# A new order of the weight stream, norm sums on VectorE, and another prelude in a hybrid decoder layer

## The reference

```python
x = x + 0.5 * swiglu_ffn(rms_norm(x, ffn1_norm), ffn1_w_gu, ffn1_w_down)      # width 5632
p = rms_norm(x, mix_norm) @ w_in       # ua, va, glu_a, glu_b, gate_a, gate_b, each 2048 wide
# A: u = gelu(ua); v = layer_norm(gelu(va)); y_a = (u * (tril(W_s) v + b_s)) @ w_pa per chunk of 128
# B: g = glu_a * sigmoid(glu_b); c = silu(layer_norm(causal depthwise conv, width 31, of g)); y_b = c @ w_pb
x = x + (sigmoid(gate_a) * y_a + sigmoid(gate_b) * y_b) @ w_out
x = x + 0.5 * swiglu_ffn(rms_norm(x, ffn2_norm), ffn2_w_gu, ffn2_w_down)
y = rms_norm(x, final_norm)            # rms_norm(x, g) = x * rsqrt(mean(x*x) + eps) * g
```

## Time and profile before

| | before |
|---|---|
| time, median of 3 runs | 3491.16 us (3490.33 to 3492.99) |
| profiled execution, its own time | 3496.27 us |
| its span, first to last instruction of the slowest core (core 2) | 3494.7 us |
| spans of the 8 cores | 3480.9 to 3494.7 us |
| PE busy | 3253.0 us (93%), 21555 matmuls |
| DVE busy | 856.9 us (25%) |
| ACT busy | 466.4 us (13%), 29 table loads |
| transfers | 284.30 MB, mean 81 GB/s |
| mean granted clock of TensorE, core 2 | 0.966 |

### The profile page before, as it was taken

The page is one execution under the profiler, slowest core; times in us unless marked ns, Lnnn a source line. Parts: engine busy times, 40 slices in busy tenths (PEclk is TensorE's granted clock), DMA queues, the critical chain, the costliest instruction groups (busy, mean ns, idle before and its releaser), DMA issues.

```text
span 3494.7 us, 51300 instructions; the slowest of 8 cores (3480.9 to 3494.7 us)
## 1 busy us (share of the span) xinstructions
PE 3253.0 (93%) x21555; PEld 2067.1 (59%) x21556; DVE 856.9 (25%) x1448; ACT 466.4 (13%) x909; POOL 128.1 (4%) x246
## 2 busy tenths in 40 slices
PE   6999999999999756579899999999999999999997
PEld 2566666666665434347756666666666666666664
DVE  2212122121126221222643111112412112112115
ACT  3000000000003100014721000000300000000002
POOL 0000000000000000000000000000000000000000
PEclk9999999999999878789999999999999999999998
DMA  6436434334345343352344334337333434434434
GB/s 155 74 61 123 80 59 81 69 66 85 66 103 127 67 85 55 78 115 59 65 87 73 71 70 71 71 69 177 58 72 71 84 63 78 73 58 82 73 63 119
DMA packets 74112, 284.30 MB, mean 81 GB/s; under 512 B 9888, under 2 KB 36768, under 8 KB 52000
## 3 DMA queue, kind: packets, MB, share of 16 engines
q0 software_dynamic: 34848, 216.62, 35.6%
q1 hardware_dynamic: 39040, 64.40, 6.3%
HBM read 468.14 MB, written 32.87 MB: 143 GB/s over the span
## 4 chain that ended last, share of the span: by engine, by line
PE 91%; DMA 5%; DVE 2%; ACT 1%; issue 1%; POOL 0%; SPq 0%; DVEq 0%; ACTq 0%; POOLq 0%
PE ps L192 91%; DMA arena<-w_glu 4%; ACT arena L195 1%; DVE arena L205 1%; DMA arena<-xin 1%; ACT L195 0%; DVE arena L209 0%; DVE arena L198 0%; DMA vsamp<-arena 0%; DMA arena<-gd 0%; POOL arena L949 0%; DMA gd<-arena 0%; SPq L949 0%; DVEq L940 0%; DVE arena L201 0%
## 5 line engine op out<-in xcount | busy, mean ns | idle before, releaser
L192 PE MATMUL ps<-arena 128*128 128x364 bf16 (+5 forms) x21555 | 3253.0, 313 | 220.7 <-DMA arena<-w_glu 141.6
L192 PEld LDWEIGHTS ps<-arena 128*128 128x128 bf16 (+1 forms) x21556 | 2067.1, 98 | 1406.5 <-issue 282.4
L198 DVE TENSOR_TENSOR arena<-arena,ps 128x364 bf16<-128x364 f32 (+9 forms) x472 | 237.0, 515 | 1838.9 <-PE ps L192 1836.4
L195 ACT ACTIVATE arena<-ps 128x364 f32<-128x364 f32 (+1 forms) x528 | 241.5, 463 | 2574.4 <-PE ps L192 2524.5
L205 DVE SCALAR_TENSOR_TENSOR arena<-ps,arena 128x364 f32<-128x364 f32 (+5 forms) x451 | 241.1, 539 | 501.2 <-PE ps L192 500.9
L198 DVE TENSOR_TENSOR arena<-arena 128x512 bf16<-128x512 f32 (+7 forms) x168 | 185.3, 1115 | 67.3 <-PE ps L192 44.2
L195 ACT ACTIVATE arena<-arena 128x364 bf16<-128x364 f32 (+6 forms) x276 | 152.8, 631 | 268.5 <-PE ps L192 191.7
L205 DVE SCALAR_TENSOR_TENSOR arena<-arena 128x364 bf16<-128x364 f32 (+4 forms) x196 | 101.2, 594 | 1.8 <-DVE arena L209 0.2
L949 POOL DMA_DIRECT2D arena<-w_gu x88 | 46.6, 529 | 1173.3 <-PE ps L192 1132.8
L949 POOL DMA_DIRECT2D arena<-w_dn x64 | 33.8, 528 | 773.8 <-PE ps L192 761.6
L195 ACT ACTIVATE arena<-ps,arena 128x272 bf16<-128x272 f32 (+3 forms) x76 | 38.0, 500 | 102.9 <-PE ps L192 102.8
(11 more groups left out here) (10 smaller groups left out, 15.9 us busy)
## 6 DMA issues: line engine op xcount, KB each, us to landing
arena<-w_gu POOLq DMA_DIRECT2D x88, 1024.0 KB, 8.1
arena<-w_dn POOLq DMA_DIRECT2D x64, 704.0 KB, 6.2
arena<-w_glu POOLq DMA_DIRECT2D x16, 1024.0 KB, 11.7
arena<-w_gate POOLq DMA_DIRECT2D x16, 1024.0 KB, 8.7
arena<-w_pab POOLq DMA_DIRECT2D x16, 1024.0 KB, 9.8
arena<-w_v POOLq DMA_DIRECT2D x8, 1024.0 KB, 9.6
arena<-w_u POOLq DMA_DIRECT2D x8, 1024.0 KB, 8.1
arena<-w_out POOLq DMA_DIRECT2D x8, 1024.0 KB, 10.3
```

The source lines that it names most:

```text
L192: return P.op("pe", lambda e: e.matmul(out, lhsT, rhs, start=start, stop=stop), deps)
L195: return P.op("act", lambda e: e.activation(out=out, in_=in_, func=func, **kw), deps)
L198: return P.op("dve", lambda e: e.tensor_tensor(out=out, in0=in0, in1=in1, op=op), deps)
```

## The change

Three parts. (1) `wseq` lists all weight tiles in the order of use, `wissue` issues the next one, `wnext` hands out the oldest issued one, and `wdone` releases a slot and issues the next tile at once, at that place of POOL's list. (2) The mixer's, the second FFN's and the final norm use `RowNorm`: each row is squared on ACT as soon as it is made, and DVE adds the squares into ACC (f32); before the last row the sum is split into two bf16 parts, which two matmuls against ONES sum over the partitions, and the last row's square is a third one. The 16 scalings stand in `norm_rows`, as before. (3) In the prelude segment 1's tokens are loaded behind segment 0's, the weight loads wait for other pieces of the tokens, `warm` puts small matmuls ahead of segment 0's sums and 30 behind them, the first unit of each segment interleaves gate and up matmuls (`paced`), and the order of the first nine units is another.

```diff
-        def wload(src, n, after=()):
-            idx, slot, free = wring.get()
-            ev = P.dma("pool", slot[:, 0:n], src, "w%d" % idx, deps=free + list(after))
-            return idx, slot, ev
+        def wissue(after=()):
+            if wseq:
+                src, n = wseq.pop(0)
+                idx, slot, free = wring.get()
+                wahead.append((idx, slot, P.dma("pool", slot[:, 0:n], src, "w%d" % idx, deps=free + list(after))))
+        def wnext():
+            return wahead.pop(0)
+        def wdone(idx, events):
+            wring.release(idx, events)
+            wissue()
...
         load_tokens(0)
         ev_pv = P.dma("sp", PV, pv_d, "c_pv")
+        load_tokens(1, [x_ev[(0, 3)]])
+        def warm(n):
+            bi, bk, bfree = banks.get()
+            lm = None
+            for i in range(n):
+                lm = mm(bk[:, 0:128], ONES, ONES, True, True, deps=[e_ones] + (bfree if i == 0 else []))
+            banks.release(bi, [lm])
...
+                    if nwarm:
+                        warm(nwarm)
                     lm = mm(bk[:, 0:n], ONES, sq[:, 0:n], k == 0, k == KC - 1, deps=[ea, e_ones] + bfree)
...
+        class RowNorm:
+            def add(self):
+                if not self.sqs:
+                    return
+                (si, sq, ea) = self.sqs.pop(0)
+                if self.ev is None:
+                    self.ev = ts(self.acc, sq, 1.0, 0.0, ALU.mult, ALU.add, deps=[ea])
+                else:
+                    self.ev = tt(self.acc, self.acc, sq, ALU.add, deps=[ea, self.ev])
+                SQR.release(si, [self.ev])
+            def row(self, k, dep):
+                self.add()
+                self.square(k, dep)
+            def split(self):
+                e1 = ts(hi[:, 0:n], self.acc, 1.0, 0.0, ALU.mult, ALU.add, deps=[self.ev] + hf)
+                e2 = tt(lo[:, 0:n], self.acc, hi[:, 0:n], ALU.subtract, deps=[e1] + lf)
+            def sum_parts(self):
+                l1 = mm(bk[:, 0:n], ONES, hi[:, 0:n], True, False, deps=[e1, e_ones] + bfree)
+                l2 = mm(bk[:, 0:n], ONES, lo[:, 0:n], False, False, deps=[e2])
+            def finish(self):
+                lm = mm(self.bank[1][:, 0:self.n], ONES, sq, False, True, deps=[ea])
+                norm_rows(gidx, Xs, Hout, self.x0, self.n, s, self.bank, lm, out)
...
                     for s in range(3):                        # last three down tiles, held
                         for (mp, wi, slot, lev) in held:
                             for mi in range(2):
-                                ld, ed = down(W, mp * 2 + mi, mi, s, lev)
-                                if s > 0:
-                                    run_steps(tail_steps[s - 1], 3)
+                                m = mp * 2 + mi
+                                if m == 10 and s == 0:
+                                    for q in range(3):
+                                        norms[q].add()
+                                if m == 15:
+                                    norms[s].add()
+                                    norms[s].split()
+                                ld, ed = down(W, m, mi, s, lev)
+                                if m == 15:
+                                    norms[s].sum_parts()
+                                    norms[s].square(m, ed)
+                                else:
+                                    norms[s].row(m, ed)
+                                if s > 0 and m == 10:
+                                    norms[s - 1].finish()
...
             if what == "w":
-                return [] if i == 0 else [x_ev[(i - 1, 3)]]
-            if what == "wl" and i < 2:
-                load_tokens(i + 1, [ev])
+                return [x_ev[((0, 1), (1, 1), (1, 3))[i]]]
+            if what == "w4":
+                return [x_ev[(2, 1)]]
+            if what == "wl" and i == 1:
+                load_tokens(2, [ev])
...
         run_steps(steps1[0], 99)
-        ffn(w_gu1, w_dn1, SEG_A, H, HID1, X1, h1, {1: steps1[1], 2: steps1[2]}, stepsm, DN_SEG, x1f, hook1,
-            [(0, 0), (0, 1), (1, 0), (1, 1), (0, 2), (1, 2), (2, 0), (2, 1), (2, 2)])
+        warm(30)
+        ffn(SEG_A, H, HID1, X1, h1,
+            {(1, 0): (lambda: run_steps(steps1[1], 99), None),
+             (1, 2): (None, lambda: run_steps(steps1[2], 99))},
+            normm, DN_SEG, x1f, hook1,
+            [(0, 0), (1, 0), (0, 1), (1, 1), (0, 2), (1, 2), (2, 0), (2, 1), (2, 2)])
...
         for c in range(SKEW, KC):                             # GLU steps
-            wi, slot, lev = wload(w_glu[c], 4096)
+            wi, slot, lev = wnext()
             la = None
             for s in range(3):
-                la = glu_unit(c, slot, lev, s, [])
-            wring.release(wi, [la])
+                la = glu_unit(c, slot, lev, s)
+            wdone(wi, [la])
             glu_out(c)
             glu_in()
             for cc in order.get(c, [c - 1]):
                 conv(cc)
```

More of the change, by code:

```diff
@@ L267, in finish @@
             def finish():
[L268 to L276, removed]
@@ L282, in run_steps, with ffn, unit @@
                 steps.pop(0)()
-        def ffn(w_gu, w_dn, segs, Hv, HID, Xs, hready, seg_steps, tail_steps, dn_seg, x_final, hook, first_order):
+        def ffn(segs, Hv, HID, Xs, hready, prep, norms, dn_seg, x_final, hook, first_order):
             hid = {}
             hid_free = {0: None, 1: None, 2: None}
-            def unit(slot, lev, jj, s, steps):
+            def unit(slot, lev, jj, s, paced=False, mid=None):
                 x0, n = segs[s]
@@ L355, in ffn @@
                                 x_final[(s, mp * 2 + mi)] = ed
-                    wring.release(wi, [ld])
+                                norms[s].row(mp * 2 + mi, ed)
+                    wdone(wi, [ld])
                 hook("g", gi)
@@ L454, in build_program, with glu_unit @@
         x1_dead = []
-        def glu_unit(c, slot, lev, s, steps):
+        def glu_unit(c, slot, lev, s):
             x0, n = SEG_A[s]
@@ L550, in conv @@
             cn_ev[c] = r
-        held = [wload(w_glu[c], 4096) for c in range(SKEW)]
+        held = [wnext() for c in range(SKEW)]
         for s in range(3):
@@ L871, in build_program @@
         h2 = {}
[L872 removed]
+        norm2 = [RowNorm(PV_F2, X2, H2, SEG_B, s, h2) for s in range(3)]
         def out_unit(W, mi, m, s, lev):
@@ L891, in build_program @@
                     lm = out_unit(wk(slot), mi, mp * 2 + mi, s, lev)
-            wring.release(wi, [lm])
-        held = [(mp,) + wload(w_out[mp], 4096) for mp in range(8 - OUT_SEG, 8)]
+                    norm2[s].row(mp * 2 + mi, x2f[(s, mp * 2 + mi)])
+            wdone(wi, [lm])
+        held = [(mp,) + wnext() for mp in range(8 - OUT_SEG, 8)]
         for s in range(3):
@@ L896, in build_program @@
                 for mi in range(2):
-                    lm = out_unit(wk(slot), mi, mp * 2 + mi, s, lev)
-                    if s > 0:
-                        run_steps(steps2[s - 1], 3)
+                    m = mp * 2 + mi
+                    if m == 10 and s == 0:
+                        for q in range(3):
+                            norm2[q].add()
+                    if m == 15:
+                        norm2[s].add()
+                        norm2[s].split()
+                    lm = out_unit(wk(slot), mi, m, s, lev)
+                    if m == 15:
+                        norm2[s].sum_parts()
+                        norm2[s].square(m, x2f[(s, m)])
+                    else:
+                        norm2[s].row(m, x2f[(s, m)])
+                    if s > 0 and m == 10:
+                        norm2[s - 1].finish()
                 if s == 2:
-                    wring.release(wi, [lm])
-            if s > 0:
-                run_steps(steps2[s - 1], 99)
+                    wdone(wi, [lm])
         x3f = {}
         yf = {}
-        stepsf = {s: rms_steps(PV_FIN, X2, None, SEG_B, s, lambda s_, k: x3f[(s_, k)], yf) for s in range(3)}
+        normf = [RowNorm(PV_FIN, X2, None, SEG_B, s, yf) for s in range(3)]
         def hook2(what, i, ev=None):
             return []
-        ffn(w_gu2, w_dn2, SEG_B, H2, HID2, X2, h2, {1: steps2[2]}, stepsf, 3, x3f, hook2,
+        ffn(SEG_B, H2, HID2, X2, h2, {(0, 1): (norm2[2].finish, None)}, normf, 3, x3f, hook2,
             [(s, jj) for s in range(3) for jj in range(SKEW)])
-        run_steps(stepsf[2], 99)
+        normf[2].finish()
         for s in range(3):
```

141 lines of the change are left out of this document (95 added, 46 removed).

## The result

The changed kernel takes 3357.2 us (median of 4 runs, 3356.2 to 3357.7) against 3491.2 before; the ratio is 0.9615, 95% interval 0.9596 to 0.9634. The forecast was 3356. The profiled execution is one of 3357.73 us, its slowest core is core 0 with a span of 3356.2. In some executions the cores of one die show a lower granted clock and take some per cent longer; all times and ratios here leave these out. The experiments ran on three chips, each together with the kernel before, so each is compared by its ratio to the kernel before on the same chip.

A forecast was written before the change was run, and what follows sets the result against it. Gapless matmuls bound the kernel, except the GLU and convolution stage, bound by late weight loads. Weight stream -169.1, what is late next +5, norms +35, prelude -6: -135 from 3491.2, so 3356 us, own range 3335 to 3380.

The forecast's parts named there:

- weight stream, full-clock work in the conv stage: GLU and convolution stage: eleven waits for w_glu go, steps take 19.92 us at full clock; gain 169.1 us.
- what is late next there: Conv stage: three small charges for cache load, last convolution's wait and a slipped step; +5 us, between 0 and +25.
- norms in FFN1's tail, with the clock: FFN1 down projection's last part: PE stalls 21.8 us for DVE, net of saved matmuls and gaps +13, before the clock.
- norms in the output projection, with the clock: Output projection's last part: PE stalls 13.8 us for DVE, net +5.5 us before the clock.
- norms in FFN2's tail, with the clock: End of the kernel: tail takes 66.5 us instead of 59.5, +7 us before the clock.
- prelude: First nine units: done at 106 us against 111.8; -6 us, between -14 and +6.
- charge for convolution 0: Start of conv stage: its cache load stands behind three weight loads; 0 to 8 us, 2 taken.
- The wait before the last convolution: End of conv stage: the 8.6 us wait may grow where a weight load leaves ahead of its gd write; 2 taken.
- The clock's part: Norm tails: idle stretches lower the clock, some 2.1 us lost after a wait; +10 us for five of six stalls.
- (a): Norm tails: DVE is in time, no stall, the norms pay as meant; 3299 us; chance 0.14.
- (b): Conv stage: SP becomes the bound, period 25.2 instead of 19.9 us; about 3410 us; chance 0.13.
- (c): Conv stage: something on POOL still precedes the weight load, the 11 waits stay; 3520 us, slower; chance 0.03.

The follow-up runs named there:

- next_only: Changed kernel, but in GLU steps 4 to 15 each weight load is issued right ahead of its own step, as before: 3505 to 3518 us, ratio 1.0033.
- late_issue: Changed kernel, but in GLU steps 3 to 15 the next weight load is issued behind the convolution and its cache load, three tiles ahead: 3355 to 3356 us, ratio 0.9612.
- paced: Changed kernel, but a norm's 16 scalings go one or two behind each unit of the next segment, not in one block: 3332 and 3333 us, ratio 0.953.
- stream_only: Kernel before with the weight stream alone (wseq, wissue, wnext, wdone), norms and prelude as before: 3338 and 3339 us, ratio 0.9564.
- no_warm: Changed kernel without the small matmuls ahead of and behind segment 0's sums: 3354 to 3356 us, ratio 0.9612.

## Why the prediction was right

The total came out within 2 us of the time, partly by luck. The mechanism of each term was right and its size within 5 us, but the errors cancel: the conv stage came out 4.8 us worse than said, the norms 8.5 better, the prelude 2.1 better. And the medians hide some of what is left: by the profiled spans the change gives 138.5 us, not 134, since the traced execution of before lies 5 us above its median. Term by term:

| step | said | measured |
|---|---|---|
| weight stream, full-clock work in the conv stage | -169.1 | eleven waits gone, steps 20.02 us apart (19.92 said) |
| what is late next there | +5 | +9.8 (so -159.3, where -164.1 was said): 6.4 us of waits at the first convolutions, the low clock after them, and 0.1 us a step |
| norms in FFN1's tail, with the clock | +17 | +13.3 |
| norms in the output projection, with the clock | +10 | +7.3 |
| norms in FFN2's tail, with the clock | +9 | +6.9 |
| prelude | -6 | -8.1 |
| rest | 0 | +1.4 (0.3 before the last convolution, 1.1 up to the output projection's tail) |
| sum | -135 | -134 by the medians, -138.5 by the profiled spans |

**The weight stream** was right in mechanism and price, and next_only put most of the price back from the other side: 3516 was said, 3505 to 3518 came, 3503 by the ratio. One reason was put too widely. I said that the load goes ahead of the convolution and four tiles ahead, as if both mattered; late_issue shows that the second alone does, and that three tiles are enough.

**What is late next.** The sample of the new order in the old trace was a true one: 9.7 us for the gd write, some 4 us to spare, no gap. Mis-sized was the charge for convolution 0, 2 us said, 6.4 us of waits measured. I had looked at the cache load and at one gd write; what was late were the gd writes of three tiles, two of them 13 to 14 us in flight behind weight loads that left 5.3 us apart, and they held SP. The wait before the last convolution was to grow by 2 and grew by 0.3.

The Trainium skill's rule (DMA: Bandwidth & Descriptors, Queues, rings and completion order), by which a DMA engine takes its queues in turn packet by packet, did not show as a short wait for the small write: 8.7 to 10.4 us in the steps with one convolution here, 10.2 for the cd write in late_issue, 2.2 to 3.8 us where no load had left in the 10 us before. Going by the row was right. Whether the engines do take turns and the small write is slow for another reason, no run shows.

**The norms.** Place and cause of the new waits were as described, in all six places, and paced shows the cause. The waits were 10.37, 7.97, 6.51, 5.18, 10.37 and 8.28 us, 48.7 together, where 55 were said; the drains and adds follow each other at 0.89 us a pair, not at the 1.07 that I took from two durations, since each starts before the one ahead of it has ended. The clock's part was right in size: the unit after the wait of 10.37 us lost 2.2 us, 2.1 were said.

**The prelude** gave 8.1 to 9.7 instead of 6. One step failed: the first unit waited for its weights and not for the scalings (25.55 instead of 24.5), and still ended at 32.2 (32.7 said), since it then ran at PE's own pace, 6.65 us for 32 matmuls. The others came as said within 1 us: segment 1's scalings began at 45.3 (46 said), the nine units ended at 103.8 (103.3 said before the allowance for the clock). The 2 to 3 us allowed for the low clock were not needed. The small matmuls, for which the prediction kept both signs open, changed nothing beyond the noise.

The rivals: that the norms pay (a) is refuted by stream_only and paced; that SP becomes the bound (b) by the 255.6 us without a gap; that the waits stay (c) by the list of waits, and next_only, which is that case, came out near the price of 3520 (3505 to 3518, 3503 by the ratio).

## What to carry to other kernels

A prefetch ring is only as deep as the issuing queue allows: a load that waits for compute, standing ahead of the next weight load, takes all distance from a ring of four slots. Issue a load where its slot comes free, and if you want to hold it back, give it an event to wait for; a later line in the program does not delay it. And before work is moved from a busy engine to an idle one, ask what stands in the idle engine's order ahead of the result that the busy one will wait for: 117 matmuls (18 us) were saved here for 51 us of waits, and both versions came out equal once the block of scalings was spread.

## What the runs showed of the hardware that was not expected

A small write issued about 1 us behind a 1 MB weight load took 8.7 to 10.4 us instead of the 2.2 to 3.8 where none had left in the 10 us before, and 13 to 14 us when loads had left every 5.3 us ahead of it (changed kernel, conv stage). That holds for whichever write happens to be next, gd or cd (late_issue). On DVE a drain and an add of 364 columns follow each other in 0.89 us though each is shown with 0.53. And 110 small matmuls ahead of the first unit changed nothing that could be measured: what the unit waited for was its weight load, and with them as without them it began at half the full pace, 0.30 us a matmul. The granted clock alone does not tell that: in no_warm it reads 1.00 over this stretch, so it is the distance between matmuls that has to be read as well.
